# Two seams of a transformer trunk: gated additions ahead of low halves and of a scale column, and four column crossings moved

## The reference, cut to what matters

```
c_act = silu(c)
for layer in range(2):
    mod = c_act @ w_ada[layer] + b_ada[layer]                 # 1024 -> 6 * 1024
    shift_m, scale_m, gate_m, shift_f, scale_f, gate_f = split(mod, 6)
    h = rms_norm(x, g_mix[layer]) * (1 + scale_m) + shift_m
    x = x + gate_m * token_mixer(h, ...)                      # ... @ w_out at its end
    h = rms_norm(x, g_ffn[layer]) * (1 + scale_f) + shift_f
    y = swiglu(h, ...) if layer == 0 else moe_swiglu(h, ...)  # dense: d_ff 2560; 8 experts, top 2, d_ff 3584
    x = x + gate_f * y
return rms_norm(x, g_final)
```

## Time and profile before

| what | value |
|---|---|
| runs of the kernel | 1579.81 to 1581.0 us, median 1580.5 |
| profiled execution: span from first to last instruction | 1578.7 us |
| median of the runs above that span | 1.8 us |
| busy: TensorE matmul, VectorE, ScalarE | 1488.8, 1297.0, 952.1 us |
| chain that ended last | TensorE 88%, VectorE 6%, ScalarE 4% |
| mean granted TensorE clock | 0.978 |
| seam A: end of the last w_out product to start of the transposes | 179.07 to 187.25 us |
| seam B: end of the last down product to start of the transposes | 364.12 to 374.09 us |

### The profile page before, as it was taken

How to read it: one execution, slowest core, us unless ns; L and a number is a source line. 1 busy time by engine, 2 the same in 40 slices (tenths; PEclk the granted TensorE clock), 3 DMA queues, 4 the chain that set the end, 5 groups by cost and what they waited for, 6 DMA issues and landing times.

```text
span 1578.7 us, 20138 instructions
## 1 busy us (share of the span) xinstructions
PE 1488.8 (94%) x7418; PEld 1224.5 (78%) x7418; DVE 1297.0 (82%) x1149; ACT 952.1 (60%) x889; POOL 5.0 (0%) x33
## 2 busy tenths in 40 slices
PE   2988899999997799999999999999999999999996
PEld 2867799998876587777878878878777787887885
DVE  6977888877677688888798798888888879879886
ACT  1645343334363577767677677677776767767764
POOL 0000000000000000000000000000000000000000
PEclk9998899998998899999999999999999999999998
DMA  9962599894613599999989989989999999998990
GB/s 336 328 240 81 174 338 324 310 323 141 219 49 119 192 359 367 323 338 360 338 318 366 348 319 363 356 299 357 366 329 333 365 337 315 380 334 323 361 363 31
DMA packets 203881, 466.58 MB, mean 296 GB/s; under 512 B 8734, under 2 KB 10940, under 8 KB 203836
## 3 DMA queue, kind: packets, MB, share of 16 engines
q1 hardware_dynamic: 203836, 465.98, 81.9%
HBM read 464.90 MB, written 1.05 MB: 295 GB/s over the span
## 4 chain that ended last, share of the span: by engine, by line
PE 88%; DVE 6%; ACT 4%; issue 2%; DMA 1%; SPq 0%; DVEq 0%; ACTq 0%
PE bank L1240 25%; PE bank L1242 25%; PE bank L1241 25%; PE bank L1562 2%; PE bank L1608 2%; ACT hgf L654 1%; DVE w_lo L1155 1%; DVE ring_sum L799 1%; ACT w_hi L666 1%; PE bank L1576 1%; PE bank L1283 1%; PE bank L1261 1%; PE bank L1440 1%; DMA raw<-in_w_ada 1%; PE bank L1418 1%
## 5 line engine op out<-in xcount | busy, mean ns | idle before, releaser
L1155 DVE TENSOR_TENSOR w_lo<-raw,w_hi 128x2048 fp32r<-128x2048 f32 x336 | 762.3, 2288 | 144.6 <-ACT w_hi L666 139.2
L666 ACT ACTIVATE w_hi<-raw 128x2048 fp32r<-128x2048 f32 x336 | 639.7, 1921 | 217.3 <-PE bank L1242 217.3
L1240 PE MATMUL bank<-w_hi,hg_hi 128*128 128x512 f32 x896 | 363.5, 406 | 7.0 <-DVE w_lo L1155 6.6
L1241 PE MATMUL bank<-w_lo,hg_hi 128*128 128x512 f32 x896 | 354.7, 396 | 0.0
L1242 PE MATMUL bank<-w_hi,hg_lo 128*128 128x512 f32 x896 | 354.7, 396 | 0.0
L1240 PEld LDWEIGHTS bank<-w_hi,hg_hi 128*128 128x128 f32 x896 | 168.7, 188 | 55.5 <-issue 10.0
L1242 PEld LDWEIGHTS bank<-w_hi,hg_lo 128*128 128x128 f32 x896 | 168.7, 188 | 40.9
L1241 PEld LDWEIGHTS bank<-w_lo,hg_hi 128*128 128x128 f32 x896 | 169.0, 189 | 36.2
L467 ACT ACTIVATE w_hi<-raw 128x2048 fp32r<-128x2048 f32 (+1 forms) x54 | 102.3, 1897 | 131.1 <-PE bank L1242 122.0
L1240 PE MATMUL bank<-w_hi,e_hi 128*128 128x512 f32 x448 | 177.9, 397 | 0.0
L1242 PE MATMUL bank<-w_hi,e_lo 128*128 128x512 f32 x448 | 177.2, 395 | 0.0
(11 more groups left out here) (245 smaller groups left out, 1527.5 us busy)
## 6 DMA issues: line engine op xcount, KB each, us to landing
raw<-in_w_ex_gate SPq DMA_DIRECT2D x112, 1024.0 KB, 6.2
raw<-in_w_ex_up SPq DMA_DIRECT2D x112, 1024.0 KB, 6.8
raw<-in_w_ex_down SPq DMA_DIRECT2D x112, 1024.0 KB, 6.5
raw<-in_w_ada SPq DMA_DIRECT2D x48, 1024.0 KB, 7.0
raw<-in_w_in SPq DMA_DIRECT2D x12, 1024.0 KB, 6.7
raw<-in_w_ff_gate SPq DMA_DIRECT2D x10, 1024.0 KB, 6.8
raw<-in_w_ff_up SPq DMA_DIRECT2D x10, 1024.0 KB, 6.6
raw<-in_w_ff_down SPq DMA_DIRECT2D x10, 1024.0 KB, 6.4
```

The source lines that it names most:

```text
L666: act_e.activation(w_hi[:, (S0 + j) % SPLIT, :], raw[:, (N0 + j) % RAW, :], ACT.Copy).then_inc(hi_done, 1)
L1155: dve.tensor_tensor(w_lo[:, sl, :], raw[:, (N0 + j) % RAW, :], w_hi[:, sl, :].bitcast(F32), ALU.subtract).then_inc(lo_done, 1)
L1240: mm(o, lh, rh, start=first, stop=False, skip_group_check=True)
L1241: mm(o, lh, rl, start=False, stop=False, skip_group_check=True)
```

## The change

The additions to x in seam A now come both ahead of the wait for crossing 9 and the gain column. In seam B the additions follow the gate at once; the two low halves go behind them, one ahead of the variance and one between the mixer's shift and gain and the operand's split. Crossings 12 to 15 stay in bank 2; 16 to 19 go to bank 7, which the FFN's products hold until x is added: 16 and 17 after x, ahead of the transposes, 18 and 19 behind the transposes. The FFN's shift and gain of layer 1 are formed later, ahead of the latent variance. Sums into `ff_sum` take its slots in reverse, so that rows 16 to 19 lie where layer 1 writes late. The sums 20 and 21 wait for the crossings that last read their slots (8 and 9).

```diff
--- before.py
+++ after.py
@@ -101,6 +101,10 @@
     IN_FF = range(10, 20)
     ada_units = [(l, c, half) for l, c in chunks for half in range(2)]
     FF_FIRST = 3
+
+    cross_order = [*range(24)]
+    crossed_at = {r: i + 1 for i, r in enumerate(cross_order)}
+    sum_before = {r: {20: 8, 21: 9}.get(r, r - 2) for r in range(24)}
 
     ff_ada = {j: 1 for j in range(FF_FIRST, len(ff_order) - 1) if j % 4}
     ff_ada[FF_FIRST] = 2
@@ -771,7 +775,7 @@
 
             def gate_half(b, r, gate, half, bias, biases):
 
-                dve.wait_ge(crossed, r + 1)
+                dve.wait_ge(crossed, crossed_at[r])
                 dve.wait_ge(bias_in, 16 * biases)
                 c = slice(half * 512, (half + 1) * 512)
                 dve.tensor_tensor(gate[:, c], bias, bank[b][:, :], ALU.add).then_inc(gate_done, 1)
@@ -788,9 +792,9 @@
                 if r not in IN_FF:
                     dst = ring_sum[:, r % 2, :]
                     if r >= 2 and half == 0:
-                        dve.wait_ge(crossed, r - 1)
+                        dve.wait_ge(crossed, crossed_at[sum_before[r]])
                 else:
-                    dst = ff_sum[:, r - IN_FF.start, :]
+                    dst = ff_sum[:, IN_FF.stop - 1 - r, :]
                 for k in range(4):
                     ck = cols2[:, 4 * half + k:4 * half + k + 1]
                     if half == 0 and k == 0:
@@ -866,19 +870,24 @@
                     lo(s); s += 1
                     rotation_angles()
                 else:
+                    lo(s); s += 1
                     variance([(0, 2, D)])
                     normalise(4 * l)
 
-                    dve.wait_ge(crossed, IN_FF.stop)
-                    for i in range(2):
-                        mod_shift(1, i, 2, 2 * KD * i)
-                        mod_gain(1, i, 2, 2 * KD * i + KD)
+                    dve.wait_ge(crossed, crossed_at[15])
+                    mod_shift(1, 0, 2, 0)
+                    mod_gain(1, 0, 2, KD)
+                    lo(s); s += 1
                     split_operand(m, hf)
                     lo(s); s += 1
                 for _ in range(2):
                     lo(s); s += 1
                     sum_unit()
 
+                if l == 1:
+                    dve.wait_ge(crossed, crossed_at[19])
+                    mod_shift(1, 1, 7, 0)
+                    mod_gain(1, 1, 7, KD)
                 variance([(0, 2, QL), (2, 4, KVL)])
                 dve.wait_ge(rstd_done, 4 * l + 2)
                 if l == 0:
@@ -1017,9 +1026,9 @@
                 for c in range(2):
                     add_gated(gate_m, (ends["out", l, 0], ends["out", l, 1]), {0: 5 * l + 1, 2: 5 * l + 2},
                               lambda i: probs[:, i, :], (c,))
-                    if (l, c) == (0, 0):
-                        dve.wait_ge(crossed, 10)
-                        mod_gain(0, 1, 0, 0)
+                if l == 0:
+                    dve.wait_ge(crossed, crossed_at[9])
+                    mod_gain(0, 1, 0, 0)
                 if l == 1:
                     for half in range(2):
                         gate_half(half, RM + 2 + half, gate_f, half, gate_f[:, half * 512:(half + 1) * 512], 4)
@@ -1057,8 +1066,6 @@
                     for half in range(2):
                         gate_half(half, 10 + half, gate_f, half, gate_f[:, half * 512:(half + 1) * 512], 2)
 
-                    lo(s); s += 1
-                    lo(s); s += 1
                     dve.wait_ge(gate_done, 4)
                     add_gated(gate_f, (ends["down", FC - 1],) * 2, {0: 3, 1: 4, 2: 5},
                               lambda i: act[:, 2 * i:2 * i + 2, :].rearrange("p a t -> p (a t)"))
@@ -1253,7 +1260,7 @@
 
 
                 pe.wait_ge(vec_used, 2 * r + 2)
-                src = ff_sum[:, r - IN_FF.start, :] if r in IN_FF else ring_sum[:, r % 2, :]
+                src = ff_sum[:, IN_FF.stop - 1 - r, :] if r in IN_FF else ring_sum[:, r % 2, :]
                 if c0 is None:
                     last = mm(bank[b][:, :], ones[:, :], src, start=True, stop=True)
                 else:
@@ -1341,14 +1348,21 @@
                 normed += 2
                 if l > 0:
 
-                    for n in range(8):
+                    for n in range(4):
                         across(12 + n, 2, 4 * n)
-                    pe.wait_ge(mod_done, 8)
+                    pe.wait_ge(x_done, 8)
+                    across(16, 7, 0)
+                    across(17, 7, 4)
+                    pe.wait_ge(mod_done, 6)
                     transposes(m, normed)
+                    across(18, 7, 8)
+                    across(19, 7, 12)
                 rows_product(0, LAT, m)
                 rows_product(2, 512)
                 columns_half(4, 0)
                 across(RM, 6)
+                if l == 1:
+                    pe.wait_ge(mod_done, 8)
 
                 pe.wait_ge(latn_done, 4 * (l + 1))
                 pe.wait_ge(lat_done, 2 * (l + 1))
```

## The result

The changed kernel is slower: 1583.68 us median (1582.21 to 1589.12, 22 runs) against 1580.60 (1579.02 to 1585.67, 22 runs) for the kernel before, ratio 1.0021, 95% interval 1.0015 to 1.0028. The forecast was 1577.0 us, range 1574.6 to 1580.4.

What follows compares the result with a forecast made beforehand. The prediction took TensorE, busy 1488.8 us or 94% of the span, to bound the kernel. Seam A's -1.7 and seam B's -1.8 gave -3.5: span 1578.7 to 1575.2, plus 1.8 for the median, 1577.0 us, range 1574.6 to 1580.4.

Steps and rivals of the forecast that it cites:

- Seam A, additions ahead of the column: -1.7: From w_out into layer 0's FFN: x complete 3.3 us earlier, of which 1.7 us reach the norm and transposes.
- The loss named with its bound: At layer 0's FFN start: products starting before the clock is back run 2.0 us at half rate, losing 0.8; bound -0.1.
- Seam B, transposes 3.9 us earlier: From layer 0's FFN into layer 1: with two crossings moved behind them, transposes start at 370.15 instead of 374.09.
- Rival 2: At both seams, an early clock fall makes each crossing moved from seam B's front save 1.7 us: 1575.6 us, chance 0.15.
- I take the middle: Layer 1's first products start at 376.4, between 375.6 and 377.3, instead of 377.66: -1.2 us.
- I expect the clock back by then: Layer 1's first products no longer run at half clock, as they did for 1.34 us: -0.6 us.
- a term of -1.8: From layer 0's FFN into layer 1: earlier products (-1.2) and their full clock (-0.6) together; bounds -3.5 and +4.0.
- rival 3: Layer 1's first products: crossings behind the transposes keep the clock at 0.50 for 10.2 us; 1582.8 us, chance 0.07.
- Nothing behind the seams depends on absolute time, so the lead stays to the end.: From behind both seams to the end: the whole -3.5 us stays, so the span goes from 1578.7 to 1575.2.
- a shift at 400 us differing from the shift at the end: Sign of being wrong, from layer 1 to the end: each later landmark should be shifted by one constant.
- Transfers, low halves, columns, reversed slots: nothing.: Around seam B and layer 1: later loads, low halves and columns are covered, reversed slots change addresses only; cost nothing.
- The median of runs is nearer the middle than any single one.: At seam B: single executions give anything between bounds -3.5 and +4.0, the median of runs lies nearer the middle.

Runs made afterwards that it cites:

- b_only: The changed kernel with seam A's edit (w_out into layer 0's FFN) undone, so only seam B's part stays: 1583.68 us, ratio 1.0012 to the kernel before.
- a_only: The kernel before with only seam A's edit, both halves of x added ahead of the wait for crossing 9 and the gain column: 1582.84 us, ratio 1.0012.
- held_before: The kernel before with dummy products behind both attentions, at seam A (26), the router and the expert's start, none at seam B: 1575.93 us, ratio 0.9966.
- front1819: The changed kernel with crossings 18 and 19 ahead of the transposes again, in bank 7 with 16 and 17: 1580.71 us, ratio 0.9992 to the kernel before.
- dense1819: The changed kernel with crossings 18 and 19 beside crossing 20 in layer 1's products, their columns formed behind them: 1579.15 us, ratio 0.9985 to the kernel before.
- a_delay4: The kernel before with seam A's edit and four useless VectorE copies that restore the old spacing there: 1580.37 us, ratio 0.9995 to the kernel before.
- before_delay1: The kernel before with one useless VectorE copy of 0.46 us at seam A, without the edit: 1583.63 us, ratio 1.0021.
- before_again: The kernel before, unchanged, traced a second time: 1579.91 us in one execution.
- a_delay2: The kernel before with seam A's edit and two useless VectorE copies, transposes 7.28 us after the last product: 1583.04 us, ratio 1.0015 to the kernel before.
- warm_before: The kernel before with dummy products behind each attention, behind layer 0's w_out and behind each of crossings 12 to 19: 1584.34 us, ratio 1.0022.
- best: The changed kernel with crossings 16 to 19 beside crossing 20 and dummy products in the gaps, also behind crossings 12 to 15: 1575.03 us, ratio 0.9966.
- held_a_undone: The changed kernel without seam A's edit, crossings 18 and 19 inside layer 1's first products, dummies (26 at seam A) everywhere but seam B: 1573.95 us, ratio 0.9956.
- best2: The changed kernel with crossings 18 and 19 inside layer 1's first products, dummies everywhere but seam B: 1570.44 us, ratio 0.9930 to the kernel before.

## Why the prediction was wrong, step by step

- *Seam A, additions ahead of the column: -1.7.* Right: x complete 3.3 us earlier, the cast next, transposes 1.82 earlier. The loss named with its bound came true in part: the products started 2.1 us before the clock was back (0.8 us of loss was priced), and the FFN's start gave 0.65 of the lead back. That was left out of the sum.
- *Seam B, transposes 3.9 us earlier.* The step is right where the clock falls late (5.78 us after the last down product in b_only, 6.03 predicted) and mis-sized in the changed kernel (7.75), where it fell after 2.2 us. Rival 2's arithmetic for an early fall was close, 11.8 us for eight crossings; from the last down product on a_only took 11.3 and held_before 11.5.
- *"I take the middle", and "I expect the clock back by then": -1.2 and -0.6.* Both failed. Crossings 18 and 19 ran at 0.50, and behind them the clock stayed there for 4.8 us of products. The first product came 0.93 us later instead of 1.2 earlier, and up to layer 1's attention another 1.59 us went instead of 0.6 won: +2.5 for a term of -1.8. This is rival 3, held at 0.07, which was priced with 10.2 us of products and +4.0. front1819 and dense1819, which differ from the changed kernel in the place of 18 and 19 and, the latter, of their columns, are 3.0 and 4.5 us faster than it.
- *"Nothing behind the seams depends on absolute time, so the lead stays to the end."* **This is the other step that failed**, and it turns even the right one into a loss. a_only has only the step that was right, and lost 2.5 us. Its lead of 1.8 us at seam A was gone in places that its edit does not touch: the FFN's start (+0.68), seam B (+2.21), w_out of layer 1 (+1.10), the router (+1.39); layer 1's first products gave 0.56 back. a_delay4 with the lead taken out again is back at 1580.37, and before_delay1, a delay without the edit, costs as much as the change. Of the 6.5 us between the predicted -3.5 and the traced +3.05, seam B and the products behind it make 4.3, the two places behind layer 1's attention 1.7, seam A with the FFN's start 0.5. The text had said that a shift at 400 us differing from the shift at the end would prove it wrong; in the changed kernel it grew by 1.70 us between layer 1's attention and the end (+0.66, +1.04).
- *Transfers, low halves, columns, reversed slots: nothing.* Nothing against it. In TensorE's waits behind seam B no transfer appears; the longest that the change could have touched, on a low half, was 2.8 us at the expert's start, where before has 2.7. front1819 has these parts of the change too and takes the time of the kernel before.
- *"The median of runs is nearer the middle than any single one."* The Trainium skill (TensorE: Matmul & The Clock Gate, section "Part 1: The HAM clock gate") has the gate's watch running free of the kernel, so that slow matmuls vary from run to run. The trace agrees in layer 0, where the fall was at 112.8 in one run and 108.8 in another, and does not bear out what I took from it: in layer 1 the same two runs had their falls, counted from the work ahead of them, within 0.11 us of each other. The median did not go to the middle between the bounds: each spacing has its own places and its own usual loss, though single runs leave it, as a_delay4's profiled one did.

Why the places repeat can be read from one pair of traces, and is not tested beyond it. Work at half clock until a given instant covers half the distance, so such a stretch halves the difference that two runs brought to it. The returns of the clock come 0.50 us earlier in before_again than in the kernel before, at 122.5, 156.6, 190.8 and 378.5 us. Its matmuls come 0.10 us earlier at 100 us, 0.30 behind the first of these stretches, 0.42 behind the second: from 0.40 apart to 0.20 to 0.1. There it stays through the third and the fourth. Open are why the clock came back late in a_delay4's execution, and why layer 1's attention is hit in a_delay2, warm_before, best and held_a_undone and not in the kernels before and after.

## What to carry to other kernels

Where TensorE has idle stretches of several microseconds, a delay of 0.5 us or a lead of 1.8 us can cost 2.5 to 3.5 us, part of it hundreds of microseconds later, by putting float32 matmuls into a stretch at half clock. One profiled execution can differ from its kernel's median in just these stretches, so take medians of a dozen runs beside the trace. So price an edit with the clock held up by dummy products in the idle time behind it, and look at the granted clock over every later seam before the edit itself is blamed. Two crossings between transposes and the first dense products cost 4.5 us more here than inside the products; and idle time ahead of float32 transposes, router products and gathers was worth filling (5.1 us in the kernel before; 8.7 from dense1819 to best2, by medians of two series), but not time between crossings on the critical path (warm_before, 4 us lost).

## What the runs showed of the hardware

- The granted clock fell under crossings that kept TensorE busy without a gap: in a_only it was 0.65 and 0.50 over two microseconds in which TensorE's busy time was 1.00 and 1.00.

```profile
364.00:365.00 1.00, 1.00 (x8) 1.00 (x8) 0.96 (x3) 0.17 (x1) 0.00 (x0) 0.65 0.09 16
365.00:366.00 1.00, 1.00 (x7) 1.00 (x6) 0.96 (x2) 0.98 (x2) 0.00 (x0) 0.50 0.01 4
```

- At clock 1.00 and 0.50: sixteen float32 transposes 1.94 us (best2, seam A) and 3.65 (before, seam A), a crossing about 0.9 and 1.6 (before, seam B). Partly at 0.50: sixteen router products 5.24 us with 3.3 of it at 0.50 (a_only) against 3.61 at 1.00 (before), thirty-two gather products 6.54 us with 5.7 of it at 0.50 (before) against 3.84 at 1.00 (best2).
- One copy of 0.46 us raised the median of twelve runs by 3.4 us (1583.63 against 1580.20 on the same chip).
- In the traces of before and before_again the clock fell 1.25 and 1.14 us behind layer 1's attention and 4.87 and 4.78 us behind its w_out, though the falls at seam A were 2.0 and 5.3 us behind the last product.
